# Retention kept in DRAM per chunk and partition, in a decoder step on one NeuronCore

## The reference, cut to what matters

```python
def retention_chunk_scan(q, k, v, log_gamma, s0, chunk):
    ...
    def step(S, inp):
        qc, kc, vc = inp
        o_inter = jnp.einsum('bhtk,bhkv->bhtv', qc, S) * q_decay
        scores = jnp.einsum('bhtk,bhsk->bhts', qc, kc) * intra_decay[None]
        o_intra = jnp.einsum('bhts,bhsv->bhtv', scores, vc)
        S_new = chunk_decay * S + jnp.einsum('bhsk,bhsv->bhkv', kc * k_decay, vc)
        return S_new, o_inter + o_intra

def odd_mixer(h, pos, w_in, w_out, s0, chunk):
    q, k, v, g = jnp.split(h @ w_in, SPLITS_ODD, axis=-1)
    q = rotary(q.reshape(b, t, H_C, DK_C), pos)
    k = rotary(k.reshape(b, t, H_C, DK_C), pos) * (DK_C ** -0.5)
    ...
    o, s_new = retention_chunk_scan(q, k, v, log_gamma, s0, chunk)
    o = rms_norm(o).reshape(b, t, W_C) * jax.nn.silu(g.astype(f32))
    return o.astype(h.dtype) @ w_out, s_new
```

## Time and profile before

| | us |
|---|---|
| median of 3 executions | 2404.05 |
| lowest, highest | 2403.65, 2407.23 |
| the profiled execution, its own time | 2409.47 |
| its span in the profile | 2407.8 |
| TensorE busy | 2076.3 |
| VectorE, GpSimd, ScalarE busy | 953.1, 712.7, 545.4 |
| mean DMA rate | 115 GB/s |

### The profile page before, as it was taken

One profiled execution on the slowest core, in us unless ns is written; L12 is line 12 of the kernel. 1 busy time (PEld: TensorE's weight loads), 2 busy tenths in 40 slices (PEclk: granted clock), 3 DMA queues, 4 the chain that ended last, 5 costly groups with the idle time before them and its releaser, 6 DMA issues. The chain is left out here.

```text
span 2407.8 us, 29437 instructions
## 1 busy us (share of the span) xinstructions
PE 2076.3 (86%) x10330; PEld 1607.4 (67%) x10330; DVE 953.1 (40%) x1374; ACT 545.4 (23%) x1032; POOL 712.7 (30%) x646
## 2 busy tenths in 40 slices
PE   5999999677778838759769999999995999995999
PEld 4789998544435437647569998877883555554786
DVE  5630000477764478832184441110001666664110
ACT  3211100355553343321130000001111333332000
POOL 3422320255550055411052242223301433325000
PEclk9999999788889967869879999999996999997999
DMA  4332221532314541134342233222214656557321
GB/s 129 112 94 74 99 86 43 153 94 88 94 54 136 157 149 47 48 107 157 112 136 91 73 114 100 83 81 83 92 47 148 220 199 236 197 209 232 111 71 34
DMA packets 229184, 276.28 MB, mean 115 GB/s; under 512 B 24420, under 2 KB 175396, under 8 KB 226916
## 3 DMA queue, kind: packets, MB, share of 16 engines
q1 hardware_dynamic: 161604, 183.79, 24.6%
q10 hardware_dynamic: 65024, 82.34, 9.6%
q0 software_dynamic: 2464, 8.91, 1.1%
HBM read 186.91 MB, written 88.08 MB: 114 GB/s over the span
## 5 line engine op out<-in xcount | busy, mean ns | idle before, releaser
L231 PE MATMUL odd_bank<-odd_w_hi,odd_h_hi 128*128 128x512 f32 (+1 forms) x576 | 224.5, 390 | 1.1 <-DVE odd_stage_tm L437 1.1
L231 PE MATMUL odd_bank<-odd_w_lo,odd_h_hi 128*128 128x512 f32 (+1 forms) x576 | 224.4, 390 | 0.0
L231 PE MATMUL odd_bank<-odd_w_hi,odd_h_lo 128*128 128x512 f32 (+1 forms) x576 | 224.1, 389 | 0.0
L1676 PE MATMUL out_bank<-out_w_hi,out_m_hi 128*128 128x512 f32 (+1 forms) x432 | 136.9, 398 | 50.9 <-DVE out_w_lo L1746 44.5
L212 POOL CAST odd_w_hi<-odd_raw 128x1024 fp32r<-128x1024 f32 x48 | 53.5, 1115 | 397.7 <-PE odd_bank L231 333.9
L1676 PE MATMUL out_bank<-out_w_hi,out_m_lo 128*128 128x512 f32 (+1 forms) x432 | 135.8, 396 | 0.0
L1676 PE MATMUL out_bank<-out_w_lo,out_m_hi 128*128 128x512 f32 (+1 forms) x432 | 135.5, 396 | 0.0
L231 PE MATMUL odd_bank<-odd_h_hi,odd_w_hi 128*128 128x362 f32 (+1 forms) x384 | 127.5, 332 | 1.5 <-DVE odd_h_lo L408 1.5
L1676 PEld LDWEIGHTS out_bank<-out_w_hi,out_m_hi 128*128 128x128 f32 (+1 forms) x432 | 80.3, 187 | 72.0 <-issue 44.8
L231 PE MATMUL even_bank<-even_h_hi,even_w_hi 128*128 128x362 f32 (+1 forms) x384 | 126.1, 328 | 1.5 <-DVE even_stage_tm L437 1.5
L231 PE MATMUL odd_bank<-odd_h_lo,odd_w_hi 128*128 128x362 f32 (+1 forms) x384 | 127.2, 331 | 0.0
(11 more groups left out here) (283 smaller groups left out, 4355.5 us busy)
## 6 DMA issues: line engine op xcount, KB each, us to landing
odd_raw<-in_w_in_odd SPq DMA_DIRECT2D x48, 512.0 KB, 3.8
even_raw<-in_w_in_even SPq DMA_DIRECT2D x32, 512.0 KB, 3.9
k_page<-in_cache_k SPq DMA_DIRECT2D x64, 256.0 KB, 3.1
v_page<-in_cache_v SPq DMA_DIRECT2D x64, 256.0 KB, 3.0
rt_s<-in_state_ret SPq DMA_DIRECT2D x32, 512.0 KB, 7.4
out_ret_sample<-rt_s ACTq DMA_DIRECT2D x32, 512.0 KB, 4.8
v_tm<-odd_stage_tm ACTq DMA_DIRECT2D x64, 128.0 KB, 1.9
g_tm<-odd_stage_tm ACTq DMA_DIRECT2D x64, 128.0 KB, 1.9
```

The costliest lines, as they stand in the source:

```text
L231: mm = pe.matmul(out, stationary, moving, start=(j == 0), stop=(j == len(pairs) - 1))
L1676: mm = pe.matmul(bank[slot][n][0:r, :], m, w[:, c, n * 512:n * 512 + 512], start=(c == 0 and j == 0), stop=(c == K - 1 and j == 2))
```

## The change

**Layout.** `by_chunk` lays a tensor of F rows out as chunk, partition, head, row block, token, with the samples' tokens behind. It is used for `q1_fm`, `k1_fm` and `mix1`. A chunk of q or k is 4 KB in a piece for each partition, a head's mix 2 KB at the store, and a tile of the output projection's load 8 KB. A head of the projection is now stored by three DMAs, two of 8 pieces of 512 bytes for a partition and one for the samples.

**Retention.** The function is written anew. The 32 steps are unrolled on all engines. TensorE computes scores two steps ahead. The samples' outputs of all four heads lie in one bank `os_`, 32 partitions for each head, for four samples at a time, so they are one unit of norm, gate and transpose for four chunks (`units`). A sample's queries are laid into `qz` once; its 8 products (16 instructions) are done in the step h = 2, with 32 columns of weights each, in four column groups of the array. The three split products for the sample's state become one: high and low parts are stacked along the contraction (24 rows: high-high, high-low, low-high) in `k_stack` and `v_stack`, by six DMAs for a sample on ScalarE's queue in the step h = 1. The keys' scaled copy `kd` is gone: both its parts are made from the transposed keys in PSUM. In the first chunk nothing is multiplied by the zero state. Semaphores for q and k, v, and g are apart, SyncE's order of loads is new, and the entrance goes over the four sample heads together. Products, sizes and precision of what remains are the same.

```diff
+def by_chunk(x):
+    full = x.rearrange("f t -> (f t)")
+    nh, nr = (HC, x.shape[0] // (HC * P))
+    prompt = full[0:x.shape[0] * TP].rearrange("(c p h r t) -> h c p r t", p=P, h=nh, r=nr, t=P)
+    sample = full[x.shape[0] * TP:].rearrange("(p h r t) -> h p r t", p=P, h=nh, r=nr)
+    return prompt, sample
...
-                    act.dma_start(place(it * 2 + s), stage_rot[:, s, :, :]).then_inc(left_fm[s], 16)
+                    whole = place(0).tensor.ap()
+                    head = (it * 2 + s + (at["fm"] if at["fm"] < HC else at["fm"] - HC)) % HC
+                    prompt, sample = by_chunk(whole)
+                    for part in range(2):
+                        act.dma_start(prompt[head, :, :, part].rearrange("c p t -> p c t"),
+                                      stage_rot[:, s, part, 0:TP].rearrange("p (c t) -> p c t", t=P)).then_inc(left_fm[s], 16)
+                    act.dma_start(sample[head], stage_rot[:, s, :, TP:T]).then_inc(left_fm[s], 16)
...
-                sp.dma_start(mix[:, slot, :, 0:r], mix_cols[:, :, bass.ds(t * P, r)]).then_inc(mix_in[slot], 16)
+                if tag == "out0":
+                    src = mix_cols[:, :, bass.ds(t * P, r)]
+                elif r < P:
+                    src = mix_sample.rearrange("h p r t -> p (h r) t")
+                else:
+                    src = mix_chunks[:, bass.ds(t, 1)].rearrange("h a p r t -> p (h a r) t")
+                sp.dma_start(mix[:, slot, :, 0:r], src).then_inc(mix_in[slot], 16)
...
-                for slot in range(2):
-                    chunk = 2 * it + slot
-                    sp.wait_ge(state_done, HC * chunk + 1)
-                    sp.wait_ge(s1_done, HC * chunk + 1)
-                    cols = bass.ds(chunk * P, P)
-                    for dst, src in ((q, q_cols), (k, k_cols)):
-                        sp.dma_start(dst[:, slot].rearrange("p h j t -> p (h j) t"), src[:, :, cols]).then_inc(chunk_in[slot], 16)
-                    sp.dma_start(v[:, slot], v_rows[cols]).then_inc(chunk_in[slot], 16)
-                    sp.dma_start(g[:, slot], g_rows[cols]).then_inc(chunk_in[slot], 16)
...
+            def load_qk(c):
+                for dst, src in ((q, q_cols), (k, k_cols)):
+                    sp.dma_start(dst[:, c % 2], src[:, c].rearrange("h p j t -> p h j t")).then_inc(qk_in[c % 2], 16)
...
+            for c in range(NCH):
+                last = HC * c + HC - 1
+                if c + 2 < NCH:
+                    sp.wait_ge(sc_done, last + 1)
+                    sp.wait_ge(kt_done, last + 1)
+                    if c:
+                        sp.wait_ge(qd_done, last + 1 - HC)
+                    load_qk(c + 2)
+                    sp.wait_ge(v_split, last + 1)
+                    load_v(c + 2)
+                if c + 1 < NCH:
+                    sp.wait_ge(os_done, c + 1)
                     for h in range(HC):
-                        sp.wait_ge(s1_done, HC * chunk + h + 1)
-                        sp.dma_start(s0[h][:], state_in[bass.ds(chunk, 1), h].rearrange("a (j k) v -> k (a j) v", k=P)).then_inc(s0_in[h], 16)
-            sp.wait_ge(state_done, NSTEP + HC + 1)
+                        sp.wait_ge(s1_done, J * (HC * c + h + 1))
+                        load_s0(c + 1, h)
+                if c + 2 < NCH:
+                    sp.wait_ge(gated, unit_of[last] + 1)
+                    load_g(c + 2)
...
+            def sample_outputs(c):
+                if c == 0:
+                    pe.wait_ge(q_set, SEQS)
+                for h in range(HC):
+                    pe.wait_ge(s0_in[h], 16 * (c + 1))
+                for j in range(J):
+                    for h in range(HC):
+                        mm = pe.matmul(os_[h * ROWS:(h + 1) * ROWS, :], qz[:, h, j, c, :], s0[h][:, j], start=False,
+                                       stop=(c % SEQS == SEQS - 1 and j == J - 1), skip_group_check=True, tile_position=(0, h * ROWS))
+                mm.then_inc(os_done, 1)
...
-                        pe.wait_ge(s0_in[h], 32 * it + 16 * slot + 16)
-                        pe.wait_ge(qx_done, n + 1)
-                        pe.wait_ge(acc_done, n + 1)
-                        for j in range(J):
-                            mm = pe.matmul(os_[:], qx[:, m, j], s0[h][:, j], start=(j == 0), stop=(j == J - 1))
-                        mm.then_inc(os_done, 1)
-                        pe.wait_ge(kx_done, 2 * n + 2)
-                        pe.wait_ge(state_done, n + HC + 2)
-                        for j in range(J):
-                            mm = product(u[j][:], (kx_hi[:, m, j], kx_lo[:, m, j]), (vs_hi[:, h], vs_lo[:, h]))
-                        mm.then_inc(us_done, 1)
...
+                pe.wait_ge(scm_split, n + 1)
+                pe.wait_ge(v_split, n + 1)
+                if n >= 2:
+                    pe.wait_ge(gated, unit_of[n - 2] + 1)
+                values = v_hi[:, i], v_lo[:, i]
+                mm = product(o[i][:], (scm_hi[:, i], scm_lo[:, i]), values, more=c > 0)
+                if c:
+                    pe.wait_ge(qd_done, n + 1 - HC)
+                    pe.wait_ge(state_done, J * (n + 1 - HC))
+                    for j in range(J):
+                        mm = pe.matmul(o[i][:], qd[:, i, j], state[:, h, j], start=False, stop=(j == J - 1))
+                mm.then_inc(o_done, 1)
+                pe.wait_ge(kd_split, n + 1)
+                for j in range(J):
+                    if n:
+                        pe.wait_ge(s1_done, J * (n - 1) + j + 1)
+                    product(u[j][:], (kd_hi[:, i, j], kd_lo[:, i, j]), values).then_inc(u_done, 1)
+                if n + 2 < NSTEP:
+                    scores(n + 2)
+                for m in turned_in(n):
+                    turn_out(m)
+                if n == GSTEP + 1:
+                    pe.wait_ge(gated, last_of[0] + 1)
+                    open_samples(1)
+                if h == 2:
+                    sample_outputs(c)
+                if h == 0:
+                    pe.wait_ge(stacked, NSTACK * (c + 1))
+                grp, rows = c // SEQS, slice(c % SEQS * ROWS, c % SEQS * ROWS + 3 * LS)
+                for j in range(J):
+                    pe.wait_ge(state_done, J * n + j + 1)
+                    pe.matmul(u[j][:], k_stack[rows, grp, h, j], v_stack[rows, grp, h], start=True, stop=True,
+                              tile_position=(c % SEQS * ROWS, 0)).then_inc(us_done, 1)
...
+            def store_state(n):
+                c, h = divmod(n, HC)
+                act.wait_ge(s1_done, J * (n + 1))
+                act.dma_start(state_samples[c, h].rearrange("(j k) v -> k j v", k=P), s1[n % 2][:]).then_inc(s1_left[n % 2], 16)
+            def stack(seq):
+                rows, grp = slice(seq * LS, seq * LS + LS), seq // SEQS
+                for part, (ks, vs) in enumerate(((ks_hi, vs_hi), (ks_hi, vs_lo), (ks_lo, vs_hi))):
+                    act.dma_start(k_stack[stack_rows(seq, part), grp].bitcast(F32), ks[rows].bitcast(F32)).then_inc(stacked, 16)
+                    act.dma_start(v_stack[stack_rows(seq, part), grp].bitcast(F32), vs[rows].bitcast(F32)).then_inc(stacked, 16)
...
+            for n in range(NSTEP):
+                if n % HC == 1 and n // HC + 1 < NS:
+                    act.wait_ge(stacked, NSTACK * (n // HC + 1))
+                    stack(n // HC + 1)
+                act.wait_ge(o_done, n + 1)
+                norm(unit_of[n], o[n % 2][:])
+                if n % GSTEP == GSTEP - 1:
+                    act.wait_ge(os_done, (n + 1) // HC)
+                    norm(last_of[n // GSTEP], os_[:])
+                if n + 2 < NSTEP:
+                    prepare(n + 2)
+                for m in turned_in(n):
+                    store(m)
+                if n:
+                    store_state(n - 1)
...
+                dve.scalar_tensor_tensor(kd_lo[:, n % 2], kt[:], k_dec[:, h:h + 1], kd_hi[:, n % 2].bitcast(F32),
+                                         ALU.mult, ALU.subtract).then_inc(kd_split, 1)
...
+            for n in range(NSTEP):
+                c, h = divmod(n, HC)
+                for j in range(J):
+                    dve.wait_ge(u_done, J * n + j + 1)
+                    if c == 0:
+                        dve.tensor_copy(state[:, h, j], u[j][:]).then_inc(state_done, 1)
+                    else:
+                        dve.scalar_tensor_tensor(state[:, h, j], state[:, h, j], gamma[h] ** P, u[j][:], ALU.mult, ALU.add).then_inc(state_done, 1)
+                if h == 0:
+                    dve.wait_ge(g_in[c % 2], 16 * (c // 2) + 16)
+                gate(unit_of[n], o[n % 2][:], g[:, c % 2, h])
+                if n % GSTEP == GSTEP - 1:
+                    dve.wait_ge(smp_g, 16 * NGRP * HC)
+                    gate(last_of[n // GSTEP], os_[:], g_s[:, n // GSTEP])
+                if n + 2 < NSTEP:
+                    prepare(n + 2)
+                dve.wait_ge(s0_in[h], 16 * (c + 1))
+                if n >= 2:
+                    dve.wait_ge(s1_left[n % 2], 16 * (n // 2))
```

(3 more changed lines are left out.)

440 lines of the change are left out of this document (207 added, 233 removed).

## The result

The changed kernel takes 2329.9 us (median of 4 runs, 2324.0 to 2334.6), where the kernel before took 2404.3 beside it: a ratio of 0.969, 95% interval 0.966 to 0.971, 74 us less. The forecast was 2301 with a range of 2272 to 2342: faster as foreseen, inside the range, 29 us short of the forecast. It also lies outside the band of 2285 to 2320, to which the prediction gave half of its chances. The profiled execution took 2327.3 us (span 2325.2), 82 less than the one before, where the sum had 103. In these terms 21 us of the sum are missing; the other 8 are scatter of the runs around the two profiled ones.

The account below looks back on a forecast made before the run. TensorE, busy for 86% of the span, was taken as the bound. Gains of 79 us in retention's loop, 17 at the entrance and 7 at the exit sum to 103, giving 2301 us on the median; range 2272 to 2342.

Parts of the forecast that it names:

- TensorE's step: Retention's loop: TensorE's own work falls from 8.55 to 6.1 us a step on average, 5.7 or 7.5 with samples' outputs.
- (a): VectorE's chain in each retention step, from state products to sample's state update: 4.85 us, hidden behind TensorE's 5.7.
- (b): ScalarE in every fourth retention step: six stacking DMAs, 2.3 to 2.5 us, delay the norm; 1.4 us, bounds 0 and 2.5.
- (c): DMA in retention: a chunk's 8.7 MB needs 23 to 25 us; two sample state buffers put a step at 6.05 us.
- The ring: Two sample state buffers in retention: each load waits for the store two steps back; a step of at least 6.05 us.
- The sum for a chunk: Four retention steps with state: 2 x 6.05 + 7.5 + 7.1 = 26.7 us; seven such chunks 187.
- Entrance: From the projection's last matmul to retention's first product: earlier start and one sample round for four; gain 17, bounds 10 and 20.
- Exit: From retention's last step to the output projection: one samples' unit, 11.3 us for 16, loads 2 us; gain 7, bounds 3 and 10.
- Transfers land late: Rival, chance 0.17: in retention's loop landings of 9 to 10 us make a chunk 30 or more; 2326 to 2335 us.
- Column groups: Rival, chance 0.07: the samples' output instructions run one after another, 6.9 in place of 1.8 us a chunk; 2342 us.
- Instruction fetch: Rival, chance 0.07: the unrolled loop's code comes in over the same DMA engines, 3 us a chunk; 2325 us.
- The title alone: Rival, chance 0.02: only the DRAM layout matters; as TensorE never waits for q or k, within 0.2%.

Follow-up runs that it names:

- e6: The changed kernel with the stack's six DMAs spread over three steps and a third buffer for the samples' new states; ratio 0.958 to the kernel before.
- e12: The changed kernel with stacking issued by SyncE, a third buffer, and the samples' norm and gate behind the next preparation; ratio 0.958 to the kernel before.
- e2: The changed kernel with only sample 0 stacked, samples 1 to 7 using its rows (wrong results); ratio 0.960 to the kernel before.
- e3: The changed kernel with ScalarE's six stacking DMAs issued two at the end of each of three steps; ratio 0.964 to the kernel before.
- e11: The changed kernel with a third buffer for the samples' new states alone; ratio 0.964 to the kernel before.
- e7: The changed kernel with SyncE stacking, third buffer, chunk 1's loads held back, and samples' norm and gate behind the next preparation; ratio 0.958 to the kernel before.

## Why the prediction was right, and where it was not

**TensorE's step: right.** 5.76 us for 5.7, and 7.6 in the step with the samples' outputs (7.5), as e6 and e12 show them undisturbed. The two stacked products take 0.65 us from the first's start to the next product's (1912.39 to 1913.04), where the sum had 0.46 and 0.3 a step for gaps; they are not 0.23 apart. The 16 instructions in column groups take 1.85 us (1904.77 to 1906.62; forecast 1.72 to 2.1), so rows with 128 moving columns did stand for 512.

**VectorE's chain (a): right.** At 1909.39 u begins, the state update at 1910.70, the first half of the sample's update ends at 1914.15, 4.76 us later (forecast 4.85). The keys' low part, read from PSUM, fell from 1.62 to 0.48 in all 32 steps:

```profile
L2170 DVE SCALAR_TENSOR_TENSOR rt_kd_lo<-rt_kt,rt_table_p,rt_kd_hi x32: 467/476/485, 1844.8 to 2070.2; 128x256 fp32r<-128x256 f32 x32
```

scm_lo stayed exposed, as the prediction had it: 0.65 beside GpSimd in the rows above, 0.29 at 1913.30 without it.

**ScalarE's stacking (b): the step that failed.** "6 x 0.38 to 0.42 = 2.3 to 2.5 us" took the price of an issue from stores of 128 partitions; the six measured 5.35. The place and the chain (norm, gate, sample's update, u) were as told. The term was 1.4 us a chunk and measured 2.1 to 2.2 (e2, e3), inside the bound of 2.5 that rested on the wrong price: 5 us too little over seven chunks. Shape alone does not give the price either: 30 of the 48 issues took 0.63 to 0.65 us, others of the same shape up to 1.46, and the 512 KB stores over 128 partitions, 0.45 at the median, up to 1.29. Another dear issue was hidden elsewhere, over 128 partitions in pieces of 256 bytes: the projection's store of the samples' columns, ns and first and last start, against 378 to 401 ns in the earlier trace rows:

```profile
L375 ACTq DMA_DIRECT2D q_fm<-odd_stage_rot x4: 1353/1462/2162, 1265.3 to 1339.7; - x4
```

**Stores (c): the right mechanism in the wrong place.** The ring was priced at 6.05 us for two steps of 5.7, 0.7 us in each of seven chunks and nothing in the first. Alone, the third buffer gave 7.5 us in the first and nothing in the seven, where the steps between the blocks keep to 5.76. That 4.9 us were forecast in all and 6.0 measured in the loop is luck. The prediction had called it VectorE's largest wait: it is 18.5 us, beside 20.0 for ScalarE's norm.

**The sum for a chunk** was 26.7 us, 187 for seven; the 28 steps measured 198.8, 12 more. e12, which has no block on ScalarE in the loop and one wait of 1.2 us for a store, shows what lies below both: 178.9. Of the 12, 5 are the stack and the stores together, 19.9 us over e12 where (b) and (c) had 14.7. 5.9 are the samples' unit in the middle (8.96 + 8.42 - 2 x 5.76), which the sum did not have at all, a step that the change put there and the walk through the code passed over. A free chunk of 24.9 where the terms gave 24.6 is 2, and the last steps, which prepare no scores, take 1.3 back. TensorE's spells at 1.2 GHz are inside the 19.9. Windows of the first four steps and of the 28, first the changed kernel, then e12:

```profile
1846.25:1882.95 36.70, 24.36 (x97) 17.29 (x95) 16.19 (x32) 11.90 (x33) 7.83 (x7) 0.69 0.91 284
1882.95:2081.79 198.84, 182.70 (x814) 113.85 (x813) 116.86 (x220) 83.76 (x225) 52.34 (x52) 0.96 0.83 272
```

```profile
1845.77:1875.71 29.94, 21.45 (x97) 15.02 (x95) 15.30 (x30) 11.59 (x32) 6.86 (x7) 0.79 0.91 281
1875.71:2054.61 178.90, 176.56 (x813) 111.05 (x812) 116.87 (x222) 84.37 (x227) 53.42 (x53) 0.99 0.90 314
```

The same instructions keep TensorE busy for 182.7 us at a mean clock of 0.96 and for 176.6 at 0.99: 6 us in the 28 steps, and 3 more in the first four, where the prediction had 3 for all spells at 1.2 GHz. The other 13.8 of the 19.9 are holes.

**The first chunk: 25 us forecast, 36.7 measured.** The 3 us for the stacking were too little: the first stack was issued by 1850.2 and landed at 1859, behind the bulk of the first loads, and TensorE waited 6.9. And the stores, to which the prediction gave nothing here, cost 7.5 (e11). With the loads held back and the third buffer (e7) the four steps take 24.6, as forecast, but the next chunk gives it back.

**Entrance: right.** The first product came at 1846.25, 20 us earlier; of these 3 lie ahead of retention (the projection's last matmul began at 1822.0 instead of 1825.0, and in other runs of these kernels anywhere from 1819.5 to 1829.3). From there to the first product it is 24.2 us for 41.1: 17, as forecast.

**Exit: the right sign, 2 us too much.** SyncE's first load comes 13.4 us after the last step (2082.9 to 2096.26; forecast 11.3, before 16.0) and the first product 18.3 later (20.65 before):

```profile
2089.42 0.58 ACT L2101 COPY rt_mix<-rt_tr 128x512 f32<-128x512 f32 x1 [4.09 <-DMA mix<-rt_mix]
2090.04 2.06 ACTq L2109 DMA_DIRECT2D mix<-rt_mix  x4
```

```profile
2096.26 0.34 SPq L1663 DMA_DIRECT2D out_raw<-in_w_out_odd  x1
```

The samples' unit waits 4.09 us for the store of a mix two units back, which the estimate of 11.3 left out.

**The rivals.** "Transfers land late" gave 2326 to 2335, and 2330 was measured, but not by its mechanism: it wanted landings of 9 to 10 us, and the stores' median stayed at 4.8. In e6 it rose to 7.2, in a kernel some 25 us faster. A rival's number that comes out is no evidence for it. Column groups did overlap. Instruction fetch took 0.2% and 0.1% of the engines' time in the loop. The loop's mean granted clock was 0.92, far from the 0.8 that would have shown the prediction wrong. Of its signs of being right, a loop of 205 to 225 us (236.7) and a DMA share over 0.85 (0.84) did not come. The title alone is worth at most 11 us of the 74, and nothing that shows inside the new loop.

The forecast of 2301 supposed a loop that nothing holds up for long; e6, with two edits more, has it: 2306.8 against 2407.9 beside it, 101 us less where the sum had 103. Its parts are not those of the sum, though: 29.4 us for the first chunk where 25 was forecast, and 183.8 for the seven where 187 was.
